# The last two stages of a two-block model kernel on one Trainium2 core: scattered gates, gathered expert rows, and a reordered scan

## The chip, the cores and the metric

The kernel runs on one core of one Trainium2 chip. The metric is the device time of one execution in microseconds (us); 5435.87 us is the median of three runs of the kernel before. All times of instructions are from one profiled execution.

## What is computed

The program is two transformer blocks on 512 tokens of width 1024. The change touches two of its nine stages. The first is the HGRN2 branch of the second block, a gated linear scan in both directions with 8 heads over 512 tokens and 256 context tokens:

```python
bc = jnp.cumsum(logf, axis=3)                       # per chunk of 64 tokens
scores = jnp.einsum('bhnid,bhnjd->bhnij', q * jnp.exp(bc - ref), k * jnp.exp(ref - bc))
o_intra = jnp.einsum('bhnij,bhnjv->bhniv', jnp.where(incl, scores, 0.0), v)
def step(S, xs):                                    # over the chunks
    o_c = einsum(qd_c, S);  S = tot_c[..., :, None] * S + einsum(kd_c, v_c)
o = _rmsnorm(o_f + _flip(o_b), norm_w) * jax.nn.silu(gate)
```

The second is `_peer`, a product-key mixture with 16,384 experts of one row each:

```python
q = (t @ w_query).reshape(n_tok, P_HEADS, 2, P_DQ)           # 8 heads, 2 halves of 128
sc = jnp.einsum('thcd,hckd->thck', q, sub_keys)              # 128 scores per half
# top 16 of each half, top 16 of their 256 sums: 16 experts a head, 128 a token
experts = (e1 * P_NKEYS + e2); gates = jax.nn.softmax(top_s)
act = jax.nn.gelu(einsum('td,tkd->tk', t, expert_u[experts])) * gates
y = einsum('tk,tkd->td', act, expert_v[experts])
```

The output is then a residual sum and an RMS norm. All is float32. Large matrix products are made with three products of float32r parts (high times high, low times high, high times low).

## The kernel before, in words

`program` runs nine phases one after the other; each is a block of five instruction streams (TensorE = PE, VectorE = DVE, ScalarE = ACT, GpSimd = POOL, SyncE = SP) that meet at semaphores. `Marks` and `Steps` are counters of named steps on one semaphore (`mark` raises it, `after` waits for it); `need` is a wait that is left out when its value isn't positive. `split_matmul` (lines 84 to 86) makes the three products.

**scan_phase** (line 2181) goes through periods; in period p it works on head p, prepares head p+1 and finishes earlier heads. On ACT: `decays` and `keys` of head p, `square_out` of head p-1, `sigmoids` of p+1, `gates` of p-1, `values` and `logs` of p+1, `log_out` of p-1, and in the next period the exponential that makes `inv`. On PE: `turn_keys` and `scores` of head p, direction 0; `outputs` of head p-1 (32 small products and 16 wider ones into the bank `out`); `turn_keys` direction 1; `updates` 0, `scores` 1, `updates` 1; `sums` of p-1; `turn_values` of p+1. On DVE: `norm` and `gated` of p-2, `decayed` (kd, ke, qe) of p, `visible` 0 (pt, qd), `states` 0 (eleven dependent steps), `visible` 1, `lengths` of p+1, `states` 1, `sums_of_logs` of p+1 in both directions. `visible` waits until `outputs` of the head before has read pt. POOL only makes constants (the semaphore `made` reaches 12) and is then idle.

**peer_phase** (line 2689) is dense: every token is multiplied with every expert, and a gate matrix of zeros and gates selects. The work is a line of units; a unit is a 128 x 1024 tile against the 1024 x 512 tokens, 8 times `split_matmul`, 24 products of 512 columns. Units 0 to 63 are 8 heads of 2 query tiles and 6 tiles of expert_u; units 64 to 143 are the other 80 tiles of expert_u; units 144 to 271 are the 128 tiles of expert_v. For each unit SP loads 512 KB into `raw` (4 slots), ACT cuts the high part (`cut`, L3112), DVE makes the low part (`low`, L2771), PE multiplies. ACT takes the result of a u unit through Gelu (L3117), and SP stores 256 KB to `hidden` in DRAM.

- Heads (units 0 to 63): after the third unit of a head PE makes the 8 score products (L3051). DVE finds the top 16 with MAX8, FIND_INDEX8 and MATCH_REPLACE8, then key numbers and gates, with eight `low`s between these steps, in an order written out by hand.
- Units 64 to 67, then a transposition of keys and gates, then units 68 to 131 with the gate matrix: for every token DVE makes two one-hot rows (L2860, L2863), PE multiplies them (L3070, 128 columns), ACT copies four tokens' results at a time into `stage` (L3157), SP stores them in 8 pieces of 4 MB to `gate_matrix`.
- Units 132 to 143 without it. SP waits for the last pieces before it loads gates.
- Units 144 to 271: SP loads per unit the v tile (512 KB), `hidden` (256 KB) and, for four units at once, the gates (1 MB). DVE multiplies hidden and gate (L2888), ACT copies the high part (L3178), DVE makes the low part (L2892), PE adds 24 products of 512 columns into eight banks.
- The end: residual (L2916), squares, 8 products with ones (L3105), mean, square root, reciprocal (L2921), output (L2923), stores.

POOL makes constants at the start of the stage and does nothing else in it. Loops run as hardware loops (`rounds`, `Fori`) on all engines.

What orders the u part is one line of the heads' loop in SP and DVE: `need(eng, cut_low, k - 3)` before the load of unit k, `need(products, k - 3)` before its cut, `need(taken, k - 3)` before its products. So a tile is loaded about four units before its use and cut about three.

## Time and profile before

| | us |
|---|---|
| median of 3 runs (5435.79 to 5437.25) | 5435.87 |
| profiled execution, its own time | 5440.96 |
| its span, first to last instruction | 5439.2 |
| PE busy in the span | 4832.4 (89%) |
| DVE busy | 3114.6 (57%) |
| ACT busy | 2083.3 (38%) |
| POOL busy | 65.8 (1%) |
| DRAM traffic, mean | 179 GB/s |

Matmuls are pipelined, so that the busy time of one (0.39 us for 512 columns) is longer than the distance between two; the distance is read from the starts in a timeline. Idle time of an engine is put down to the engine that released it.

### The profile page before, as it was taken

The numbers are of one execution on the slowest core, as the hardware profiler recorded it, in microseconds if no ns is written. First come the engines' busy times: TensorE is split into PE (matmuls) and PEld (weight loads), VectorE is DVE, ScalarE is ACT, GpSimd is POOL, SyncE is SP. The second block draws the span as 40 slices with busy tenths as digits, with TensorE's granted clock in tenths as the row PEclk, the third lists the DMA queues.
The fourth block names the chain that finished last, engine by engine and source line by source line (L and its number), as shares of the span: only waits on it lengthen the run. The fifth ranks groups of instructions, "written<-read, shape, count | busy, mean of one in ns | idle before, by whom it ended". The sixth has DMA issues, their size and how long they took to land. (4 is left out here: it accounts for less than half of the span.)

```text
span 5439.2 us, 67843 instructions
## 1 busy us (share of the span) xinstructions
PE 4832.4 (89%) x24244; PEld 3935.6 (72%) x24244; DVE 3114.6 (57%) x5040; ACT 2083.3 (38%) x2398; POOL 65.8 (1%) x137
## 2 busy tenths in 40 slices
PE   8926799999999569999799975677999999899998
PEld 3923477877877458878699965533888888788887
DVE  0062388888888642233688856512887666344444
ACT  1000267767767301111455545411333444322222
POOL 1000100000000100000000000000000000000000
PEclk9557899999999779999799986688999999999999
DMA  8412599999999623244111011142333454666663
GB/s 345 147 39 91 203 355 367 371 364 367 369 365 368 248 112 109 106 137 141 55 34 36 28 40 47 37 157 102 124 127 127 173 200 170 221 196 191 197 192 120
DMA packets 256059, 976.23 MB, mean 179 GB/s; under 512 B 27060, under 2 KB 63492, under 8 KB 202212
## 3 DMA queue, kind: packets, MB, share of 16 engines
q1 hardware_dynamic: 248516, 923.74, 47.5%
q0 software_dynamic: 7392, 50.50, 2.3%
q8 instruction: 92, 1.51, 0.1%
q14 instruction: 59, 0.48, 0.0%
HBM read 799.87 MB, written 174.28 MB: 179 GB/s over the span
## 5 line engine op out<-in xcount | busy, mean ns | idle before, releaser
L84 PE MATMUL peer_bank<-peer_t_high,peer_high 128*128 128x512 f32 x2176 | 856.4, 394 | 49.4 <-DVE peer_low L2771 35.8
L86 PE MATMUL peer_bank<-peer_t_high,peer_low 128*128 128x512 f32 x2176 | 849.9, 391 | 0.0
L85 PE MATMUL peer_bank<-peer_t_low,peer_high 128*128 128x512 f32 x2176 | 848.2, 390 | 0.0
L2771 DVE TENSOR_TENSOR peer_low<-peer_raw,peer_high 128x1024 fp32r<-128x1024 f32 x272 | 332.6, 1224 | 622.0 <-ACT peer_high L3112 622.0
L1076 DVE TENSOR_TENSOR moe_low<-moe_raw,moe_high 128x2048 fp32r<-128x2048 f32 x256 | 574.6, 2286 | 55.9 <-ACT moe_high L984 53.0
L84 PEld LDWEIGHTS peer_bank<-peer_t_high,peer_high 128*128 128x128 f32 x2176 | 409.9, 188 | 133.1 <-issue 50.6
L984 ACT ACTIVATE moe_high<-moe_raw 128x2048 fp32r<-128x2048 f32 x256 | 478.3, 1906 | 3.7 <-PE moe_up_bank L894 2.0
L3112 ACT ACTIVATE peer_high<-peer_raw 128x1024 fp32r<-128x1024 f32 x272 | 287.0, 1056 | 486.2 <-PE peer_bank L86 481.0
L86 PEld LDWEIGHTS peer_bank<-peer_t_high,peer_low 128*128 128x128 f32 x2176 | 409.5, 188 | 87.0
L85 PEld LDWEIGHTS peer_bank<-peer_t_low,peer_high 128*128 128x128 f32 x2176 | 410.0, 188 | 83.5
L1081 DVE TENSOR_TENSOR moe_low<-moe_raw,moe_high 128x2048 fp32r<-128x2048 f32 x128 | 293.0, 2289 | 66.4 <-ACT moe_high L989 66.4
L3117 ACT ACTIVATE peer_gelu<-peer_bank 128x512 f32<-128x512 f32 x128 | 76.5, 598 | 458.9 <-PE peer_bank L86 458.8
L989 ACT ACTIVATE moe_high<-moe_raw 128x2048 fp32r<-128x2048 f32 x128 | 244.3, 1909 | 0.9 <-DMA moe_raw<-w_down 0.8
L892 PE MATMUL moe_gate_bank<-moe_high,moe_x_high 128*128 128x512 f32 x512 | 210.0, 410 | 11.9 <-DVE moe_low L1076 11.9
L892 PE MATMUL moe_gate_bank<-moe_low,moe_x_high 128*128 128x512 f32 x512 | 201.1, 393 | 0.0
L892 PE MATMUL moe_up_bank<-moe_high,moe_x_high 128*128 128x512 f32 x512 | 201.1, 393 | 0.0
L894 PE MATMUL moe_up_bank<-moe_high,moe_x_low 128*128 128x512 f32 x512 | 200.8, 392 | 0.0
L892 PE MATMUL moe_up_bank<-moe_low,moe_x_high 128*128 128x512 f32 x512 | 200.8, 392 | 0.0
L894 PE MATMUL moe_gate_bank<-moe_high,moe_x_low 128*128 128x512 f32 x512 | 200.1, 391 | 0.0
L170 PE MATMUL mix_bank<-mix_silu_c,mix_ada_w 128*128 128x2 f32 x768 | 164.0, 353 | 5.2 <-ACT mix_silu_c L484 5.2
L170 PEld LDWEIGHTS mix_bank<-mix_silu_c,mix_ada_w 128*128 128x128 f32 x768 | 163.9, 333 | 6.0 <-ACT mix_silu_c L484 6.0
L77 DVE CAST zin_both_w_high<-zin_both_w 128x1024 fp32r<-128x1024 f32 x40 | 27.8, 694 | 242.5 <-DMA zin_both_w<-w_in 242.5
(535 smaller groups left out, 9170.1 us busy)
## 6 DMA issues: line engine op xcount, KB each, us to landing
moe_raw<-w_gate_up SPq DMA_DIRECT2D x256, 1024.0 KB, 6.8
moe_raw<-w_down SPq DMA_DIRECT2D x128, 1024.0 KB
peer_raw<-expert_u SPq DMA_DIRECT2D x128, 512.0 KB, 3.7
peer_raw<-expert_v SPq DMA_DIRECT2D x128, 512.0 KB, 3.5
hidden<-peer_gelu SPq DMA_DIRECT2D x128, 256.0 KB
gate_matrix<-peer_stage SPq DMA_DIRECT2D x8, 4096.0 KB, 12.3
peer_stage<-gate_matrix SPq DMA_DIRECT2D x32, 1024.0 KB, 7.6
peer_stage<-hidden SPq DMA_DIRECT2D x128, 256.0 KB, 3.4
```

The costliest lines, as they stand in the source:

```text
L84: pe.matmul(out, wh, xh, start=start, stop=False)
L85: pe.matmul(out, wh, xl, start=False, stop=False)
L86: return pe.matmul(out, wl, xh, start=False, stop=stop)
L170: last = pe.matmul(out, self.slots[:, n, c], x, **flags)
L892: pe.matmul(out[:], sh[:, c], w[:, part][:, q * 512:(q + 1) * 512], start=False, stop=False, skip_group_check=True)
L894: last = pe.matmul(out[:], sl[:, c], wh[:, part][:, q * 512:(q + 1) * 512], start=False, stop=stop, skip_group_check=True)
L984: act.activation(high[:, gu_slot[j]], raw[:, gu_slot[j]], ACT.Copy).then_inc(gu_high, 1)
L989: act.activation(high[:, dn_slot[j]], raw[:, dn_slot[j]], ACT.Copy).then_inc(dn_high, 1)
L1076: v.tensor_tensor(low[:, slot], raw[:, slot], high[:, slot].bitcast(F32), ALU.subtract).then_inc(gu_low, 1)
L1081: v.tensor_tensor(low[:, slot], raw[:, slot], high[:, slot].bitcast(F32), ALU.subtract).then_inc(dn_low, 1)
L2771: v.tensor_tensor(low_part[:, slot], raw[:, slot], high[:, slot].bitcast(F32), ALU.subtract).then_inc(cut_low, 1)
L3112: act.activation(high[:, slot], raw[:, slot], ACT.Copy).then_inc(cut_high, 1)
```

## The change

It has three parts.

1. **Scan stage.** `outputs` and `sums` of head p now run at the end of period p instead of in the middle of period p+1; `out` is copied to SBUF (`oc`) by a new ACT instruction per head, and `norm` reads that copy. PE makes `updates` 0 before `turn_keys` 1, and `turn_values` before `updates` 1; `updates` leaves out the last chunk. ACT makes `logs` before `values` and `square_out` last. DVE makes `sums_of_logs` 0 before `states` 1. POOL writes zeros to the whole of `gate_matrix`, 32 DMAs of 768 KB.
2. **Peer stage, 384 dense columns.** Expert units (256 of 272) work on the first 384 tokens. Query units keep 512. `hidden` and `gate_matrix` have rows of 384, 192 KB per tile. The one-hot rows, their products, their copies and stores are gone. Instead DVE makes, after each head's keys, the cell number of each (token, expert) pair (three small instructions: pair, cell, expert), and POOL adds each gate to its cell with an indirect DMA of 128 elements of 4 bytes: 16 x 3 per head, 384 in all. Before a head's scatters POOL waits for all scatters of the heads before. SP waits for all scatters before it loads gates.
3. **The last 128 tokens.** POOL gathers, for each of the 128 experts of a token, the row of expert_u and later that of expert_v (128 rows of 4 KB per DMA, 256 DMAs, ring of 6 buffers). DVE makes the dot product with one instruction per gathered u tile and adds a v tile times its gate with another; ACT makes Gelu. Of the 128 dots 112 stand before unit 144, spread over units 69 to 145, the other 16 in the first 16 v units; one v row stands in each v unit. At the end PE transposes the sum into the last 128 columns. The tail makes the root with Ln and Exp on ACT, without reciprocal. All loops of the peer stage are unrolled.

The core of the diff:

```diff
+DENSE = 3 * P
@@ scan_phase
+            pool.memset(zeros[:], 0.0).then_inc(made, 1)
+            for n in range(PEER_KEYS // 4):
+                pool.dma_start(d["gate_matrix"][4 * n:4 * n + 4].rearrange("m e t -> e m t"), zeros[:]).then_inc(gates_cleared, 16)
+            pool.wait_ge(gates_cleared, 16 * PEER_KEYS // 4)
...
                 AO.mark("sq", h, act.activation(sq[:], ob[:], ACT.Square))
+                AO.mark("oc", h, act.activation(oc[h % 2][:], ob[:], ACT.Copy))
...
-                if head(p - 1):
-                    square_out(p - 1)
                 if head(p + 1):
                     sigmoids(p + 1)
                 if head(p - 1):
                     gates(p - 1)
                 if head(p + 1):
-                    values(p + 1)
                     logs(p + 1)
                 if head(p - 1):
                     log_out(p - 1)
+                if head(p + 1):
+                    values(p + 1)
+                if head(p):
+                    square_out(p)
...
                 if head(p):
                     turn_keys(p, 0)
                     scores(p, 0)
-                if head(p - 1):
-                    outputs(p - 1)
-                if head(p):
+                    updates(p, 0)
                     turn_keys(p, 1)
-                    updates(p, 0)
                     scores(p, 1)
-                    updates(p, 1)
-                if head(p - 1):
-                    sums(p - 1)
                 if head(p + 1):
                     turn_values(p + 1)
+                if head(p):
+                    updates(p, 1)
+                    outputs(p)
+                    sums(p)
...
                     lengths(p + 1)
+                    sums_of_logs(p + 1, 0)
                 if head(p):
                     states(p, 1)
                 if head(p + 1):
-                    sums_of_logs(p + 1)
+                    sums_of_logs(p + 1, 1)
@@ peer_phase, DVE
+        place_u = lambda j: j if j < EARLY else EARLY + 2 * (j - EARLY) + 1
+        place_v = lambda j: EARLY + 2 * j if j < TOPK else EARLY + TOPK + j
+        due = lambda k: (k - LATER - 4) * EARLY // (VBASE - LATER - 3)
...
+                V.mark("pair", h, v.scalar_tensor_tensor(pair[:], key2[:], float(PEER_KEYS), key1[:], ALU.mult, ALU.add))
+                V.mark("cell", h, v.scalar_tensor_tensor(cell[:, :, head(h)], pair[:, 0:TD], float(DENSE),
+                                                         token[:, 0:TD].unsqueeze(2).to_broadcast([P, TD, TOPK]), ALU.mult, ALU.add))
+                V.mark("expert", h, v.tensor_copy(expert[:, head(h)], pair[:, TD]))
...
+            def dot(j):
+                n = place_u(j)
+                v.wait_ge(gathered[n % RING], 16 * (n // RING + 1))
+                v.scalar_tensor_tensor(ring[:, n % RING], ring[:, n % RING], 1.0, tok[:], ALU.mult, ALU.mult,
+                                       accum_out=dots[:, j:j + 1]).then_inc(used, 1)
+            for k in range(LATER + 5, VBASE + 2):
+                low(k)
+                for j in range(due(k - 1), due(k)):
+                    dot(j)
...
+            for m in range(PEER_KEYS):
+                if VBASE + 2 + m < LAST:
+                    low(VBASE + 2 + m)
+                if m + 2 < PEER_KEYS:
+                    low_hidden(m + 2)
+                if m + 3 < PEER_KEYS:
+                    gating(m + 3)
+                row(m)
+                if m < TOPK:
+                    dot(EARLY + m)
@@ peer_phase, SP
+                if k == VBASE:
+                    sp.wait_ge(scattered, 16 * HEADS * TOPK * TD)
+                    for m in range(4):
+                        load_gated(m)
@@ peer_phase, POOL
+            def scatter(h, k, t):
+                pool.indirect_dma_start(out=cells, out_offset=at_cell, in_=gate[:, t, h * TOPK + k:h * TOPK + k + 1], in_offset=None,
+                                        compute_op=ALU.add).then_inc(scattered, 16)
+            def gather(rows, j, n):
+                need(pool, used, n - RING + 1)
+                pool.indirect_dma_start(out=ring[:, n % RING], out_offset=None, in_=rows,
+                                        in_offset=bass.IndirectOffsetOnAxis(ap=expert[:, j:j + 1], axis=0)).then_inc(gathered[n % RING], 16)
+            for h in range(HEADS):
+                V.after(pool, "gates", h)
+                need(pool, scattered, 16 * TOPK * TD * h)
+                for k in range(TOPK):
+                    for t in range(TD):
+                        scatter(h, k, t)
+                    if h == 4 and k < RING:
+                        gather(u_rows, k, place_u(k))
+                    if h > 4:
+                        for n in range(2):
+                            j = RING + (h - 5) * 2 * TOPK + 2 * k + n
+                            gather(u_rows, j, place_u(j))
+            for j in range(RING + 6 * TOPK, EARLY):
+                gather(u_rows, j, place_u(j))
```

## Rows read from the trace of the kernel before

**Rows 1.** Windows by stage: scan, heads, rest of u, v, tail; columns in the first line.
```profile
core 0: us, PE busy (x) PEld busy (x) DVE busy (x) ACT busy (x) POOL busy (x), PEclk, DMA share, GB/s
3222.00:3549.00 327.00, 189.01 (x1440) 162.16 (x1440) 190.35 (x342) 161.57 (x240) 2.55 (x13) 0.61 0.15 49
...
3803.00:4166.00 363.00, 363.00 (x1668) 302.95 (x1667) 293.36 (x1032) 129.69 (x208) 0.00 (x0) 1.00 0.39 129
4166.00:4720.00 554.00, 540.34 (x2890) 464.15 (x2889) 331.76 (x1108) 249.52 (x291) 0.00 (x0) 0.99 0.50 178
4720.00:5416.00 696.00, 696.00 (x3068) 576.13 (x3066) 303.28 (x376) 196.61 (x249) 0.00 (x0) 1.00 0.59 188
5416.00:5440.00 24.00, 8.03 (x18) 2.46 (x16) 14.79 (x18) 6.95 (x10) 0.00 (x0) 0.76 0.23 87
```
**Rows 2.** Timeline, PE: products of 512 columns, v stage, two high-by-high ones three apart.
```profile
5000.01 0.39 PE L84 MATMUL peer_bank<-peer_t_high,peer_high 128*128 128x512 f32 x1
...
5000.69 0.39 PE L84 MATMUL peer_bank<-peer_t_high,peer_high 128*128 128x512 f32 x1
```
**Rows 3.** The same view, input stage, products of 256 columns, two apart.
```profile
2200.75 0.28 PE L84 MATMUL zin_context<-zin_hT_high,zin_both_w_high 128*128 128x256 f32 x1
...
2200.98 0.28 PE L86 MATMUL zin_context<-zin_hT_high,zin_both_w_low 128*128 128x256 f32 x1
```
**Rows 4.** DVE's longest wait in the heads' stretch, 3803 to 4166: total, times, longest.
```profile
DVE peer_tick L2790 <- PE peer_bank L3051: 36.8, 8, 4.6
```
**Rows 5.** Timeline, DVE in head 1: its first step and its gates.
```profile
3850.93 0.16 DVE L2790 TENSOR_TENSOR peer_tick<-peer_tick 128x1 f32<-128x1 f32 x1 [4.64 <-PE peer_bank L3051]
...
3887.85 0.22 DVE L2849 TENSOR_TENSOR peer_chosen<-peer_eg,peer_esum 128x64 f32 x1
```
**Rows 6.** POOL's indirect DMAs by source line: the scatters, and the gathers' landing.
```profile
L682 POOL DMA_INDIRECT rows<-route_htok,route_desti x16: 962/962/1071, 556.9 to 576.0; - x16
...
DMA to landing us min/median/max: 11.3/11.4/11.6
```
**Rows 7.** Timeline of the gathers from where DVE is busy beside them.
```profile
1877.32 5.24 DVE L1214 SCALAR_TENSOR_TENSOR combine_acc<-combine_got,combine_gates,combine_acc 128x1024 f32<-128x1024 f32 x4
1878.26 1.15 POOL L1272 DMA_INDIRECT combine_got<-expert_rows,combine_dest  x1 [0.30 <-issue]
1879.71 1.01 POOL L1272 DMA_INDIRECT combine_got<-expert_rows,combine_dest  x1 [0.30 <-issue]
1881.03 1.02 POOL L1272 DMA_INDIRECT combine_got<-expert_rows,combine_dest  x1 [0.30 <-issue]
```
**Rows 8.** A plain small DMA of POOL, by source line.
```profile
L406 POOL DMA_DIRECT2D mix_colsa<-conv_a_b x1: 554/554/554, 2.6 to 2.6; - x1
```
**Rows 9.** Timeline, from the last u unit to the first v unit.
```profile
4715.52 1.35 DVE L2888 TENSOR_TENSOR peer_stage<-peer_stage 128x512 f32<-128x512 f32 x2 [8.56 <-DMA peer_stage<-hidden]
...
4719.19 0.63 PE L84 MATMUL peer_bank<-peer_t_high,peer_high 128*128 128x512 f32 x1
```
**Rows 10.** Groups of the low part and the gating product, 3500 to 5440.
```profile
L2771 DVE TENSOR_TENSOR peer_low<-peer_raw,peer_high 128x1024 fp32r<-128x1024 f32 x272 | 332.6, 1224 | 622.0 <-ACT peer_high L3112 622.0
...
L2888 DVE TENSOR_TENSOR peer_stage<-peer_stage 128x512 f32<-128x512 f32 x128 | 87.5, 684 | 8.7 <-DMA peer_stage<-hidden 8.6
```
**Rows 11.** Windows: first block's expert stage, and beside the gathers; GB/s stands last.
```profile
900.00:1000.00 100.00, 98.28 (x448) 79.32 (x447) 88.54 (x67) 69.86 (x54) 0.00 (x0) 1.00 0.95 367
...
1863.00:1883.00 20.00, 0.00 (x0) 0.00 (x0) 5.88 (x8) 0.00 (x0) 15.19 (x16) 0.50 1.01 383
```
**Rows 12.** Timeline of one period of the scan stage.
```profile
3384.92 0.95 DVE L2507 TENSOR_TENSOR gla_kd<-gla_k,gla_e 128x768 f32<-128x768 f32 x1
...
3388.40 2.08 PE L2438 MATMUL gla_out<-gla_pt,gla_v 128*128 128x128 f32 x8
...
3395.20 0.73 DVE L2519 COPY_PREDICATED gla_pt<-gla_mask,gla_scores 128x512 f32<-128x512 uint32 x1 [5.10 <-PE gla_out L2442]
...
3422.41 0.95 DVE L2507 TENSOR_TENSOR gla_kd<-gla_k,gla_e 128x768 f32<-128x768 f32 x1
```

More of the change, by code:

```diff
@@ new lines, in peer_phase @@
+        expert = s.sb("expert", [P, HEADS * TOPK], U32)
+        tok, y = s.sb("tok", [P, D]), s.sb("y", [P, D])
+        dots, acts = s.sb("dots", [P, HEADS * TOPK]), s.sb("acts", [P, HEADS * TOPK])
+        ring = s.sb("ring", [P, RING, D])
+        tT = early[:, 0:DC * SEQ].rearrange("p (c t) -> p c t", t=SEQ)
+        gated_tiles = early[:, 0:10 * DENSE].rearrange("p (a t) -> p a t", t=DENSE)
+        hid, gates, prod = gated_tiles[:, 0:4], gated_tiles[:, 4:8], gated_tiles[:, 8:10]
+        whole = shared[:].rearrange("p (a t) -> p a t", t=SEQ)
@@ L2909, in _, with gating @@
-            rounds(v, PEER_KEYS // VG - 1, groups)
-            groups(PEER_KEYS // VG - 1, last=True)
+                V.mark("gates", h, v.tensor_tensor(gate[:, :, head(h)], eg[:], esum[:].unsqueeze(2).to_broadcast([P, TT, TOPK]), ALU.mult))
+                low(h * 8 + 12)
+            def gating(m):
+                slot = m % 4
+                v.wait_ge(gates_l[slot], 16 * (m // 4 + 1))
+                v.wait_ge(hid_l[slot], 16 * (m // 4 + 1))
+                need(v, hid_low, m - 1)
+                v.tensor_tensor(prod[:, m % 2], hid[:, slot], gates[:, slot], ALU.mult).then_inc(gated, 1)
@@ new lines, in weigh, with row @@
+            def weigh(h):
+                v.wait_ge(acted, h + 1)
+                v.tensor_tensor(acts[:, head(h)], acts[:, head(h)], gate[:, TD, head(h)], ALU.mult).then_inc(weighed, 1)
+            def row(j):
+                n = place_v(j)
+                v.wait_ge(weighed, j // TOPK + 1)
+                v.wait_ge(gathered[n % RING], 16 * (n // RING + 1))
+                v.wait_ge(used, n)
+                if j:
+                    v.scalar_tensor_tensor(y[:], ring[:, n % RING], acts[:, j:j + 1], y[:], ALU.mult, ALU.add).then_inc(used, 1)
+                else:
+                    v.tensor_scalar(y[:], ring[:, n % RING], acts[:, j:j + 1], None, ALU.mult).then_inc(used, 1)
@@ L2935, in store_u @@
[L2935 removed]
+                sp.dma_start(raw[:, k % 4], source(k)).then_inc(unit_l[k % 4], 16)
+            def store_u(k):
+                m = u_tile(k)
                 sp.wait_ge(taken, k + 1)
[L2937 to L2941 removed]
@@ L3000, in groups @@
[L3000 to L3007 removed]
+                sp.dma_start(d["hidden"][m], gel[:, m % 2]).then_inc(hid_stored[m % 2], 16)
@@ new lines, in load_gated @@
+            def load_gated(m):
+                need(sp, gated, m - 3)
+                sp.dma_start(gates[:, m % 4], d["gate_matrix"][m]).then_inc(gates_l[m % 4], 16)
+                sp.wait_ge(hid_stored[m % 2], 16 * (m // 2 + 1))
+                sp.dma_start(hid[:, m % 4], d["hidden"][m]).then_inc(hid_l[m % 4], 16)
+            sp.dma_start(tT, d["tT"]).then_inc(t_l, 16)
+            for k in range(LAST):
+                if k == VBASE:
+                    sp.wait_ge(scattered, 16 * HEADS * TOPK * TD)
+                    sp.wait_ge(tok_made, 2)
+                    for m in range(4):
+                        load_gated(m)
+                load(k)
+                if k == 1:
+                    sp.dma_start(keys, d["keysT"]).then_inc(k_l, 16)
+                if 4 <= k < VBASE + 4 and not is_query(k - 4):
+                    store_u(k - 4)
+                if k >= VBASE + 4:
+                    load_gated(k - VBASE)
+                if k == VBASE + 8:
+                    V.after(sp, "gates", HEADS - 1)
@@ L3099, in _ @@
-            groups(0, first=True)
-            with pe.Fori(1, PEER_KEYS // VG - 1) as i:
-                groups(i)
-            groups(PEER_KEYS // VG - 1, last_round=True)
+            pe.wait_ge(made, 7)
+            for c in range(DC):
+                last = pe.transpose(bank[6 + c // 4][:, c % 4 * P:(c % 4 + 1) * P], tT[:, c, DENSE:SEQ], ident[:])
+            last.then_inc(turned, 1)
+            for k in range(VBASE):
+                if k < LATER and k % 8 == 3:
+                    h = k // 8
+                    if h == 0:
+                        pe.wait_ge(k_l, 16)
+                    pe.wait_ge(taken, h * 8 + 2)
+                    V.after(pe, f"r{TT - 1}1", h - 1)
+                    for t, c in ((t, c) for c in range(2) for t in range(TT)):
+                        last = pe.matmul(score[c][:, t], qs[:, c, t * P:(t + 1) * P], keys[:, h * 2 + c], start=True, stop=True)
+                    T.mark("scores", h, last)
+                unit(k)
@@ new lines, in _ @@
+            V.after(pe, f"r{TT - 1}1", HEADS - 1)
+            pe.wait_ge(tok_made, 2)
+            for m in range(PEER_KEYS):
+                k = VBASE + m
+                slot = k % 4
+                pe.wait_ge(cut_low, k + 1)
+                pe.wait_ge(hid_low, m + 1)
+                for c in (4, 5, 6, 7, 0, 1, 2, 3):
+                    if m == 0 and c == 0:
+                        pe.wait_ge(taken, VBASE)
+                    part = slice(c * P, (c + 1) * P)
+                    last = split_matmul(pe, bank[c][:, 0:DENSE], (high[:, slot, part], low_part[:, slot, part]), (hh[:, m % 4], hl[:, m % 4]),
+                                        start=m == 0, stop=m == PEER_KEYS - 1)
+                last.then_inc(products, 1)
@@ L3115, in take_u, with take @@
+            def take(k):
                 act.wait_ge(products, k + 1)
-                need(act, hid_stored[half], m)
-                act.activation(gel[:, half], bank[slot][:], ACT.Gelu).then_inc(taken, 1)
+                if is_query(k):
+                    T.after(act, "scores", k // 8 - 1)
+                    act.activation(qs[:, k % 8], bank[k % 4][:], ACT.Copy).then_inc(taken, 1)
+                else:
+                    m = u_tile(k)
+                    need(act, hid_stored[m % 2], 16 * (m // 2))
+                    act.activation(gel[:, m % 2], bank[k % 4][:, 0:DENSE], ACT.Gelu).then_inc(taken, 1)
```

550 lines of the change are left out of this document (203 added, 347 removed).

## The prediction

> **What bounds the kernel now.** I read the windows by stage first. The v stage takes 696 us with PE busy in all of it, the heads 363 us likewise, and the rest of the u part 554 us with 540 busy, at a full granted clock of 1.00; POOL does nothing in any of them and DRAM carries 129 to 188 GB/s [rows 1]. So the peer stage is bound by PE. The scan stage is something else: no engine is busy for 60% of its 327 us, and PE's granted clock is 0.61 on average, that is, mostly its lower level of 1.2 GHz. It is a chain of waits.
>
> The timeline of PE gives the price of a product. Three of 512 columns take 5000.69 - 5000.01 = 0.68 us, 0.227 each [rows 2]; two of 256 columns take 0.23 us, 0.115 each [rows 3]. Halfway is 0.171 for 384 columns. A unit of 24 products is 5.44 us now and would be 4.1 after; I use 4.15. 256 of 272 units are shorter by 1.3 us: 333 us at most from this alone.
>
> Then I looked at what else stands in a head. DVE begins a head at 3850.93 and has its gates at 3887.85 [rows 5], 37 us of a period of 45.3 (363 / 8). Of the other 8 us it waits 4.6 for the scores, 36.8 us in 8 heads [rows 4].
>
> **The change, term by term** (against the profiled execution, span 5439.2 us, time 5440.96).
>
> *Heads.* PE needs 2 x 5.44 + 6 x 4.15 + 1.8 for the scores (45.3 - 8 x 5.44 now) = 37.6 us. DVE needs its 37 us, 0.6 for pair, cell and expert (three instructions near the 0.22 of the gates' product), 1.2 for the last low part [rows 10], and can take back the 1 us it waits for the exponentials: about 38. So PE and DVE are level, and DVE has the last word by little. 8 x 38 = 304 us instead of 363. This alone would be 59 us, if something waited for it.
>
> *POOL.* It is new in this stage, and I think it takes over as the bound. An indirect DMA is 0.96 us with 0.30 us between two; where DVE was busy beside it the starts are 1.45 and 1.32 apart [rows 6, 7]. I take 1.32 for scatters and gathers alike. The kernel before has no adding scatter and none of 4 bytes. The nearest row is the scatter of 128 rows, same number of indices, which I take. Bounds: from below the plain small DMA, 0.55 [rows 8] and no gap; from above 2 x 0.96 + 0.30 = 2.2, if an add has to write its read side twice, for source and destination.
> Up to the first v unit POOL issues 384 scatters and 112 gathers, in one line. It starts at the gates of head 0, 3805 + 38 = 3843 (3805 is where the first scores are done: 3803.4 and 1.8). 496 x 1.32 = 655 us; each head but the first waits until all scatters of the last have landed, 7 x 4 us (the gathers' landing of 11.4 us [rows 6] was behind 512 KB each, a scatter moves 512 bytes; bounds 2 and 11): 28 us. The last gather is issued at 4526. PE alone would be at the 68th unit at 3803 + 304 and at the end of the u units 77 x 4.15 later, at 4427, so POOL is late by 100 us: the gathers of heads 5 to 7 stand between the scatters, the first dot waits until POOL has done head 4 (3843 + 240 x 1.32 + 16 + 6 x 1.32 = 4184, while DVE is there by 4110), and DVE's low parts are queued behind the dots. PE then starves, unit by unit.
>
> *From the last gather to the first v unit.* Landing, the last dots, SP's loads of gates, hidden and tile, gating, high and low part. Before, DVE waits 8.6 us for these loads, and from its first gating (4715.52) to PE's first v product (4719.19) it is 3.7 us more, 12.3 in all [rows 9]. With a landing in front I take 20 (bounds 13 and 35): the v stage begins at 4546, 173 us earlier than now.
>
> *v stage.* Per unit PE 4.15. DVE: low part 1.22, two products of 384 columns at 0.55 (0.68 for 512 less a quarter of the 0.54 that 512 columns more cost) [rows 10], one v row at 1.31 (5.24 / 4 [rows 7]): 3.65. In the first 16 units a dot comes on top, 1.31 and some 0.15 for its sum: 5.1, over PE by 1 us. DRAM: tile 512, gathered rows 512, hidden and gates 192 each, 1408 KB = 1.44 MB, in 4.15 us 347 GB/s. Rates of 367 and 383 are to be had [rows 11], but with nothing left over, and here stands random 4 KB and 1.5 KB traffic. I take 16 x 5.1 + 112 x 4.25 = 558 us (bounds: 4.15 everywhere, 531; 4.8, 614), against 696. POOL issues one gather per unit, 1.3 us, hidden.
>
> *Tail.* Ends 23 us after the last product now. Reciprocal (3.35) and mean (0.7) leave, eight transposes and one more table load come: -2 us.
>
> *Scan.* Before, the outputs of the last head run from 3388.40 to 3395.1 between a head's kd and its pt, and DVE waits 5.1 us for them; a period is 3422.41 - 3384.92 = 37.5 us [rows 12]. After, they run at the end of the period, where half of them (direction 0) lies beside DVE's states; the other half, square and copy (3.2 + 0.6 + 0.6) come before ACT's next exponentials, since ACT is in order, while DVE is at the second sum of logs (3.4 us). The first sum of logs (3.4 us) moves in front of states 1, into time in which DVE waited. Following the chain through gives 32 us per period. 7 x 5.5 = 38, and some 8 at the end, where the head's outputs no longer need a period of their own. Against it stand 25 MB of zeros on POOL's queue: 25.2 MB / 367 GB/s = 69 us of the DMA engines in the first two or three periods, beside loads of 1.5 MB a period that are issued a period ahead. I charge 5. Sum -41 (bounds -15, if the new order only halves the gain; -55).
> The moved instructions leave the queue of SP as it was. POOL waits for the zeros to land, with nothing queued behind; the stage lasts 290 us, so this costs nothing. The unrolled loops cost nothing by themselves: the scan stage is unrolled already.
>
> **Sum.** v stage ends 4546 + 558 = 5104; tail 21; less 41: span 5084. The profiled time is 1.8 above its span and 5.1 above the median of the runs: 5086 - 5 = **5081 us** as a median.
>
> **A rule against it.** Beside a DVE instruction with two SBUF inputs POOL's instruction went from 0.95 to 1.15 and 1.01, never more [rows 7]. The Trainium skill (SBUF — State Buffer, Who interferes with whom) says that such an instruction and a GpSimd instruction that reads SBUF exclude each other for the whole of the instruction, and whoever comes second is blocked. By that rule the trace's 0.2 us would be a mild case; the rival "blocked" below is what it would be at full size.
>
> **Rivals.**
> 1. *The read side of the add costs* (1.5 to 2.2 us per scatter). Every 0.1 us more is 38 us, since POOL is the bound: 5150 at 1.5, 5419 at 2.2. For it: an add has to read its destination, and no row shows one. Against it: the instruction's time may go by indices, 128 in each. 0.17.
> 2. *Blocked.* If each of 496 POOL instructions waited for half of a 1.2 us DVE instruction, 0.6 x 496 = 298 us: 5379. Against it rows 7. 0.05.
> 3. *Cheaper scatters* (0.55 to 1.1). POOL leaves the path at about 1.1 us per instruction (100 us / 496 = 0.2 below 1.32), and PE and DRAM bound the u part: up to 100 us less, 4981. 0.10.
> 4. *DRAM bounds* the v stage at 300 GB/s: 4.8 us per unit, 112 x 0.55 = 62 more: 5143. For it the 347 GB/s needed, against it rows 11. 0.08.
> 5. *Slower: the adds are slow to land.* All scatters of a head have to land before the next head's. If the DMA engines make each 4-byte add by itself, reading, adding and writing before the next, each engine has 8 per scatter; at 0.4 us an add a scatter takes 3.2 us, 384 x 1.9 us over the forecast: 5810. It decides from 2.25 us per scatter. Against it: the chip moves 128-index scatters of 4 KB rows at 1.27 us each. For it: nothing in the trace reads before it writes. 0.09.
> 6. *It does not do what it says:* PE was not the bound of the v stage. Rows 1 and 2 exclude it.
>
> The forecast itself has 0.51.
>
> **Range and chances.** 4960 holds rival 3 and the better end of the scan; 5330 holds rival 4 and two thirds of rival 1. Outside stand rivals 5 and 2 and the rest of 1, about 0.19. A measurement of this kernel can tell about 0.2%, 11 us, from no change. Faster: the forecast, 2, 3, 4 and nearly all of 1: 0.89. Slower: rival 5 and the end of 1: 0.09. Same: 0.02.
>
> **What would show it.** In the changed profile: products of 384 columns 0.17 us apart; POOL with 640 indirect DMAs, without a break from 3843 less the scan's gain to the first v unit; DVE waiting for gathered rows (ring) in the u part, and PE idle behind low parts; a stall of DVE of some 70 us at the first dot; heads of 38 us; v units of 4.2 to 4.3 us after the first 16, at about 340 GB/s; periods of 32 us in the scan. It is wrong if the starts of two scatters are not 1.2 to 1.4 us apart, if DVE's heads stay at 45 us, or if the v units are near 5 us.

## The result and the profile after

The kernel after takes **5359.32 us** (median of 4 runs, 5356.09 to 5364.82), the kernel before 5436.56 in the same runs: ratio 0.9856, 95% interval 0.9841 to 0.987, 1.4% faster. The forecast was 5081 with a range from 4960 to 5330. The sign is right, the size is not: 77 us came of the 355 forecast, and the time lies above the range. The profiled execution took 5357.13 us, span 5355.4, so the sum of the prediction (5084) is short by 271 us.

The windows by stage, as in [rows 1]: heads (first scores to the gates of the last head), rest of u, v stage, tail.

```profile
core 0: us, PE busy (x) PEld busy (x) DVE busy (x) ACT busy (x) POOL busy (x), PEclk, DMA share, GB/s
...
3767.10:4070.80 303.70, 302.26 (x1669) 285.54 (x1668) 294.23 (x1054) 125.26 (x210) 214.83 (x123) 1.00 0.60 144
4070.80:4789.50 718.70, 381.12 (x1848) 364.59 (x1846) 226.93 (x314) 111.96 (x163) 582.66 (x380) 0.78 0.63 165
4789.50:5333.30 543.80, 538.20 (x3071) 537.13 (x3072) 443.25 (x541) 186.63 (x255) 227.51 (x139) 0.99 0.96 349
5333.30:5355.40 22.10, 8.94 (x27) 3.43 (x25) 10.75 (x16) 8.92 (x12) 0.00 (x0) 0.82 0.26 95
```

The heads went from 363 to 304 us and the v stage from 696 to 544, both much as forecast. The second row holds the loss: 719 us, with PE busy in 381 of them, and POOL in 583. A product of 384 columns takes what halfway between [rows 2] and [rows 3] said, 4999.67 to 5001.23 for nine:

```profile
4999.67 0.33 PE L84 MATMUL peer_bank<-peer_hidden_high,peer_high 128*128 128x384 f32 x1
...
5001.23 0.33 PE L84 MATMUL peer_bank<-peer_hidden_high,peer_high 128*128 128x384 f32 x1
```

POOL was 21% of the span busy, for 1%. By line it heads the chain that ended last (by engine PE has 13% of it and POOL 10%):

```profile
POOL gate_matrix L3015 8%; PE peer_bank L84 4%; PE peer_bank L86 4%; PE peer_bank L85 4%; POOL peer_ring L3020 2%; DMA peer_ring<-expert_u_rows,peer_expert 1%; DMA peer_raw<-expert_v 1%; DVE peer_ring L2895 1%; DMA peer_early<-hidden 0%; DVE peer_low L2794 0%; PE peer_bank L3072 0%; DMA gate_matrix<-peer_gate,peer_cell 0%; DMA peer_early<-tT 0%; DVE peer_y L2908 0%; PE peer_bank L3095 0%
```

So the first thing to look at was the price of POOL's instruction. By source line (min/median/max ns), the scatters, and the gathers of u and of v rows:

```profile
L3015 POOL DMA_INDIRECT gate_matrix<-peer_gate,peer_cell x384: 1539/1557/3802, 3805.6 to 4745.3; - x192
...
L3020 POOL DMA_INDIRECT peer_ring<-expert_u_rows,peer_expert x128: 938/997/2041, 4210.7 to 4860.5; - x128
L3020 POOL DMA_INDIRECT peer_ring<-expert_v,peer_expert x128: 938/1677/2640, 4767.0 to 5308.7; - x128
```

No scatter is under 1.54 us, where [rows 6] has 0.96. The group of them on the page of the profile gives their mean:

```profile
L3015 POOL DMA_INDIRECT gate_matrix<-peer_gate,peer_cell x384 | 656.1, 1709 | 205.8 <-issue 125.4
```

At 1.709 on the mean there must be a second effect on top; it shows in the v rows, whose median is 1.68 with a minimum of 0.94. The timeline of a head and of a v unit shows what stands beside the long ones:

```profile
3817.70 1.55 POOL L3015 DMA_INDIRECT gate_matrix<-peer_gate,peer_cell  x1 [0.30 <-issue]
3819.55 3.80 POOL L3015 DMA_INDIRECT gate_matrix<-peer_gate,peer_cell  x1 [0.30 <-issue]
3823.66 1.55 POOL L3015 DMA_INDIRECT gate_matrix<-peer_gate,peer_cell  x1 [0.31 <-issue]
...
3819.38 1.41 DVE L2829 TENSOR_TENSOR peer_shared<-peer_top 128x256 f32<-128x256 f32 x4
3820.71 1.22 DVE L2794 TENSOR_TENSOR peer_low<-peer_raw,peer_high 128x1024 fp32r<-128x1024 f32 x1
...
5000.45 1.22 DVE L2794 TENSOR_TENSOR peer_low<-peer_raw,peer_high 128x1024 fp32r<-128x1024 f32 x1
5000.81 1.68 POOL L3020 DMA_INDIRECT peer_ring<-expert_v,peer_expert  x1 [2.48 <-DVE peer_y L2908]
```

The scatter at 3819.55 is the one that has DVE's sums for the candidates and a low part beside it, with two inputs each; it ends 3.80 us later. The gather at 5000.81 starts inside a low part that hands over at about 5001.6, and ends 0.9 us after that: as if it had stood still until then. In the whole stage the 163 scatters with no DVE instruction beside them take 1.565 on the mean, the 69 such gathers 0.98.

What followed from it, in DVE's and PE's waits from 4070 to 4790 (total, times, longest):

```profile
DVE peer_ring L2895 <- DMA peer_ring<-expert_u_rows,peer_expert: 478.8, 76, 141.9
PE peer_bank L84 <- DVE peer_low L2794: 326.8, 50, 134.7
```

DVE waits for gathered rows, 142 us for the first of them, and PE behind it for low parts: the chain forecast, but twice as long.

### The profile page after: what moved, and what is told of

Its sections match the earlier page's. It is cut to its first block and busy times, and to the rows that moved or that the text cites. A ratio compares the mean times of both kernels' runs of the same rounds, so it can differ in the third digit from the quotient of the medians.

```text
span 5355.4 us, 62778 instructions
## 1 busy us (share of the span) xinstructions
PE 4472.7 (84%) x23192; PEld 3793.6 (71%) x23192; DVE 3146.1 (59%) x4430; ACT 1936.2 (36%) x2287; POOL 1117.1 (21%) x811
## 5 line engine op out<-in xcount | busy, mean ns | idle before, releaser
L3015 POOL DMA_INDIRECT gate_matrix<-peer_gate,peer_cell x384 | 656.1, 1709 | 205.8 <-issue 125.4
L84 PE MATMUL peer_bank<-peer_t_high,peer_high 128*128 128x384 f32 (+1 forms) x1152 | 421.7, 366 | 328.1 <-DVE peer_low L2794 328.0
L85 PE MATMUL peer_bank<-peer_t_low,peer_high 128*128 128x384 f32 (+1 forms) x1152 | 412.1, 358 | 0.0
L86 PE MATMUL peer_bank<-peer_t_high,peer_low 128*128 128x384 f32 (+1 forms) x1152 | 411.5, 357 | 0.0
L84 PE MATMUL peer_bank<-peer_hidden_high,peer_high 128*128 128x384 f32 x1024 | 344.7, 337 | 16.5 <-DVE peer_hidden_low L2889 16.5
L85 PE MATMUL peer_bank<-peer_hidden_low,peer_high 128*128 128x384 f32 x1024 | 344.1, 336 | 0.0
L86 PE MATMUL peer_bank<-peer_hidden_high,peer_low 128*128 128x384 f32 x1024 | 343.9, 336 | 0.0
L3020 POOL DMA_INDIRECT peer_ring<-expert_v,peer_expert x128 | 214.1, 1673 | 290.6 <-DVE peer_y L2908 280.5
L86 PEld LDWEIGHTS peer_bank<-peer_t_high,peer_low 128*128 128x128 f32 x1152 | 231.2, 201 | 5.2
L84 PEld LDWEIGHTS peer_bank<-peer_hidden_high,peer_high 128*128 128x128 f32 x1024 | 193.8, 189 | 17.9 <-issue 17.3
```

Of the source, the lines that this page charges most:

```text
L84: pe.matmul(out, wh, xh, start=start, stop=False)
L85: pe.matmul(out, wh, xl, start=False, stop=False)
L86: return pe.matmul(out, wl, xh, start=False, stop=stop)
L3015: pool.indirect_dma_start(out=cells, out_offset=at_cell, in_=gate[:, t, h * TOPK + k:h * TOPK + k + 1], in_offset=None, compute_op=ALU.add ...
L3020: pool.indirect_dma_start(out=ring[:, n % RING], out_offset=None, in_=rows, in_offset=bass.IndirectOffsetOnAxis(ap=expert[:, j:j + 1], axi ...
```

## Experiments

Each run is compared with the kernel before on the same chip. The times of after and its variants, in us, as they stand to one another:

| kernel | median | ratio to before, 95% interval | v stage starts, first product |
|---|---|---|---|
| after | 5359.3 | 0.9856 (0.9841 to 0.987) | 4789.5 |
| scatters write, not add | 5259.7 | 0.9669 (0.965 to 0.9688) | 4697.3 |
| two of three tiles scattered | 5130.2 | 0.9431 (0.9412 to 0.945) | 4561.3 |
| low part by one-input DVE instruction | 5336.2 | 0.981 (0.979 to 0.9829) | 4770.4 |
| low part by ACT | 5314.2 | 0.9767 (0.9742 to 0.9793) | 4739.1 |
| 32 early dots | 5275.6 | 0.9697 (0.968 to 0.9713) | 4656.3 |
| 64 early dots | 5311.8 | 0.9763 (0.9743 to 0.9782) | 4717.4 |
| first head plain | 5341.3 | 0.9816 (0.9798 to 0.9833) | 4778.3 |
| 32 early dots, first head plain | 5269.3 | 0.9676 (0.9658 to 0.9694) | 4652.7 |
| 24 early dots, first head plain | 5269.9 | 0.9678 (0.966 to 0.9697) | 4644.2 |

**Is it the add?** The kernel after with one argument less:

```diff
-                                        compute_op=ALU.add).then_inc(scattered, 16)
+                                        ).then_inc(scattered, 16)
```

> The 384 scatters write their gate instead of adding it (where a token has the same expert from two heads, only the last head's gate stays in the cell; all else is computed). Theory A, the add makes POOL's instruction long: a scatter falls from 1.55 us alone to about 0.96, like the scatter of the kernel before, its start-to-start time from 1.85 to about 1.3; 384 x 0.55 = 211 us leave POOL, the v stage begins near 4581 instead of 4792, and the time is about 5150. Theory B, the 4-byte row and the index into single cells make it long: 1.55 stays, and the time is 5359 within 10.

By source line:

```profile
L3015 POOL DMA_INDIRECT gate_matrix<-peer_gate,peer_cell x384: 966/972/2021, 3806.4 to 4652.3; - x192
```

Theory A holds for POOL's instruction: 0.97, and 0.979 on the mean for those with no DVE instruction beside them, against 1.565. The 4-byte row and the index into single cells cost nothing. The time fell only half as far as it expected, 5260 and not 5150, for a reason that neither theory had. The longest waits of ACT and of SP from 3806 and 3840 on, PE and ACT in the timeline of the second head, and two windows:

```profile
ACT peer_gelu L3111 <- DMA merge_pb_w<-w_pb: 283.7, 16, 49.7
...
SPq L2968 <- ACT peer_gelu L3111: 286.1, 33, 50.3
```
```profile
3929.61 0.48 PE L84 MATMUL peer_bank<-peer_t_high,peer_high 128*128 128x384 f32 x1 [2.32 <-issue]
3932.41 0.48 PE L85 MATMUL peer_bank<-peer_t_low,peer_high 128*128 128x384 f32 x1 [2.32 <-issue]
...
3945.03 0.49 ACT L3111 ACTIVATE peer_gelu<-peer_bank 128x384 f32<-128x384 f32 x1 [49.67 <-DMA merge_pb_w<-w_pb]
```
```profile
3900.00:3940.00 40.00, 7.17 (x15) 4.60 (x16) 1.35 (x7) 0.00 (x0) 29.13 (x31) 0.50 0.02 0
...
3950.00:3962.00 12.00, 12.00 (x56) 10.09 (x55) 11.79 (x19) 6.40 (x15) 0.00 (x0) 1.00 0.54 187
```

While POOL issues plain scatters in a row, one each 1.27 us, PE makes one product in 1.4 to 2.8 us: 15 of them in 40 us. These gaps lie inside a unit of 24 products, where the code waits for nothing, and the profile names no wait for them ("issue"). ACT's 50 us are the wait for such a unit's last product. The DMA that the profile puts them down to isn't the cause: no transfer is under way (0 GB/s from 3900 to 3940), and SP sends the store of a tile only after ACT's Gelu, for which it waits 286 us in all. The last scatter of the row ends at 3938; by 3945 PE's products follow one another again, and the loads and stores are back. Up to 4420 there are 88 products that start more than 1.2 us after the one before and wait for nothing, 193 us together; in the kernel after there is none. The heads' pitch of 38 us breaks (the gates of the last come at 4289, not 4071), and POOL then waits 68 us for gates and 78 for one dot. Why PE's instructions come so slowly beside plain scatters, and not beside adding ones, is open.

**Is it the add by itself, or the bytes?** The kernel before, with the 16 scatters of [rows 6] adding:

```diff
-                                            in_=htok[:, t, :], in_offset=None).then_inc(scattered, 16)
+                                            in_=htok[:, t, :], in_offset=None, compute_op=ALU.add).then_inc(scattered, 16)
```

> The kernel before, with its 16 scatters of 4 KB rows adding to the cleared rows instead of writing them (every row has one writer, so nothing changes in the result). If the add's 0.59 us is a price per instruction or per index, these go from 0.96 to about 1.55 us each and start 1.85 apart, 9 us in all; if it goes by bytes, 4 KB per index shows as far more than 2 us each. The time is 5437 within 25: beside POOL's 9 us the landing, 11.4 us, can at most double for each of the last ones.

```profile
L682 POOL DMA_INDIRECT rows<-route_htok,route_desti x16: 1557/1562/1702, 555.5 to 583.7; - x16
...
DMA to landing us min/median/max: 6.5/12.6/17.2
```

From 0.962 to 1.562, with rows a thousand times as long: the add costs POOL 0.60 us per instruction of 128 indices, whatever their size. Whether it goes by instruction or by index these runs don't tell, as all have 128. The transfers themselves are another matter. From 565 to 575, before and with the add:

```profile
565.00:575.00 10.00, 10.00 (x25) 4.50 (x24) 1.38 (x2) 0.60 (x1) 7.56 (x9) 1.00 1.00 386
...
565.00:575.00 10.00, 10.00 (x25) 4.50 (x24) 1.38 (x2) 0.60 (x1) 8.44 (x6) 1.00 1.05 207
```

The DMA engines are full in both, and carry 207 instead of 386 GB/s. One run, 5436.5 us.

**Is POOL the bound?** A third of the scatters out (`range(TD)` becomes `range(TD - 1)` in the scatters' loop, and the counts waited for with it).

> Scatters only for two of the three dense tiles of tokens, 256 instead of 384 (tokens 256 to 383 get no gates, so the product of experts for them is left out of the result; all of PE's and DVE's work stays). If POOL is the bound of the u part: 128 x 1.85 = 237 us less, the v stage begins near 4555 and the time is about 5122. Rival, the gathers and dots bound the u part by themselves (landing, ring of 6, DVE's order): under 100 us less, over 5260.

5130, and the v stage starts 228 us sooner: POOL is the bound of the u part, up to the size of this cut. The gathers and dots by themselves allow a start at 4561 or sooner.

**Does DVE hold POOL up?** Two ways to take away the two-input instruction that stands in every unit.

```diff
-                v.tensor_tensor(low_part[:, slot], raw[:, slot], high[:, slot].bitcast(F32), ALU.subtract).then_inc(cut_low, 1)
+                v.tensor_scalar(low_part[:, slot], raw[:, slot], 0.0, None, ALU.mult).then_inc(cut_low, 1)
```

> The low part of a tile is made by a DVE instruction of one SBUF input (times zero) instead of the difference of two, so the third product of each unit multiplies by zero and the result loses the low part; the schedule stays. Contention theory (POOL's indirect DMAs are held up by DVE instructions with two SBUF inputs): the gathers of the v stage, all 1.67 us now, fall to about 1.0 where no other two-input instruction is beside them; the scatters' mean falls from 1.71 towards 1.6 (the sums for the candidates stay two-input), so up to 384 x 0.11 = 42 us and for 112 gathers up to 112 x 0.3 = 34 us leave POOL, and the time is 5270 to 5330. Rival, the stretch is POOL's own or the DMA queue's and only happens to stand beside DVE: gathers stay at 1.6 to 1.7 and the time at 5359 within 10.

The group of the low part, and the v rows:

```profile
L2794 DVE TENSOR_SCALAR peer_low<-peer_raw 128x1024 fp32r<-128x1024 f32 x268 | 185.7, 693 | 23.7 <-ACT peer_high L3102 23.6
```
```profile
L3020 POOL DMA_INDIRECT peer_ring<-expert_v,peer_expert x128: 937/1147/1687, 4749.8 to 5288.4; - x128
```

The time came near to where the theory put it (5336, just above its 5270 to 5330), but not for its reason: scatters that overlap most with this instruction took 1.88 us (53 of them), no less than those beside the two-input one in the kernel after (1.87, 80 of them), and the gathers only fell to 1.15, which fits the shorter instruction. One input is thus no protection, and the run doesn't tell theory from rival. So DVE was taken out of it altogether:

```diff
                 act.activation(high[:, k % 4], raw[:, k % 4], ACT.Copy).then_inc(cut_high, 1)
+                act.activation(low_part[:, k % 4], raw[:, k % 4], ACT.Copy, scale=0.0).then_inc(cut_low, 1)
```

> The kernel after, with the low part of a tile made by ACT (a copy times zero, beside the copy for the high part) and not by DVE, so DVE's 272 two-input instructions of 1.22 us are gone in the peer stage; the third product of each unit multiplies by zero, the low part is left out of the result. The run with a one-input instruction was not clean, since that instruction took 0.69 us and still stood beside stretched gathers. Contention theory: gathers of the v stage fall from 1.64 to about 1.0 to 1.1 (the rows' own instruction and the products remain), the 80 scatters that stood beside the low part lose 26 us, the u part's gathers about 20 to 30, and the v stage begins 40 to 60 us sooner: about 5310. Rival, POOL is stretched by something else that comes at the pitch of the units (a load's DMA, PE): 1.64 stays and the time is 5359 within 10.

```profile
L3018 POOL DMA_INDIRECT peer_ring<-expert_v,peer_expert x128: 935/939/1811, 4728.1 to 5261.2; - x128
```

1.68 became 0.94 with PE and all loads as before and more work on ACT, the scatters' mean went from 1.709 to 1.654, and the time to 5314: the theory's numbers. (Of the 50 us by which the v stage starts sooner, 5 come from the first gates, which a freer DVE has ready at 3800 and not 3805.) What is left of the stretch stands beside the dots (97 scatters, 1.86 on the mean) and the heads' own two-input steps. It matters who is first: in the kernel after 42 of POOL's instructions began with DVE idle and had a two-input instruction begin beside them, and none of them took more than 0.03 us longer than one alone. The Trainium skill (SBUF — State Buffer, Who interferes with whom) names both kinds, the two-input instruction and the one-input copy in its fast mode, and says that the one that comes second is blocked and not slowed; where POOL comes second these traces agree, 1.68 for the gather that starts inside a low part. Where DVE comes second no run shows it: the 133 low parts that start inside one of POOL's instructions take 1.22 us, like the 21 with none beside them. And they differ in one thing: the page takes `tensor_tensor` to spare a GpSimd that makes descriptors, and here it doesn't.

**Fewer gathers in front of the v stage.** `EARLY` says how many of the 128 dots come before it.

```diff
-    RING, EARLY = 6, 7 * TOPK
+    RING, EARLY = 6, 2 * TOPK
+    LATE = HEADS * TOPK - EARLY
...
-    place_v = lambda j: EARLY + 2 * j if j < TOPK else EARLY + TOPK + j
+    place_v = lambda j: EARLY + 2 * j if j < LATE else EARLY + LATE + j
...
-                if m < TOPK:
+                if m < LATE:
                     dot(EARLY + m)
...
-                    if h == 4 and k < RING:
+                    if h == 3 and k < RING:
                         gather(u_rows, k, place_u(k))
-                    if h > 4:
-                        for n in range(2):
-                            j = RING + (h - 5) * 2 * TOPK + 2 * k + n
-                            gather(u_rows, j, place_u(j))
+                    j = RING + ((h - 4) * TOPK + k) // 2
+                    if h > 3 and k % 2 and j < EARLY:
+                        gather(u_rows, j, place_u(j))
```

> Only 32 of the 128 dots (and their gathers) stand before the v stage, the other 96 go one by one into its first 96 units. If POOL is the bound: from its start at 3805 it has 384 x 1.85 = 710 us of scatters, 28 of waits between heads and 32 gathers of about 1.6, 51 us; with 15 us for landing and loads the v stage begins near 4610 (4792 now). The v stage then takes 96 x 4.63 + 32 x 4.17 = 578 us (541 now), and the time is about 5210. Rival, DRAM can't carry 1.97 MB per unit at 4.63 us (425 GB/s): at 400 GB/s a unit is 4.9 us, at 350 5.6 us, and the time 5240 to 5300. Rival, POOL is not the bound: the v stage begins no earlier than 4750, and the time is over 5350.

```profile
4557.00:4656.00 99.00, 0.53 (x4) 0.21 (x2) 6.13 (x9) 3.41 (x6) 70.11 (x48) 0.53 0.38 75
4656.00:5117.00 461.00, 425.48 (x2304) 400.26 (x2304) 421.70 (x575) 142.74 (x199) 277.75 (x188) 0.99 1.03 407
5117.00:5252.00 135.00, 134.21 (x769) 132.78 (x768) 110.07 (x133) 44.86 (x62) 53.60 (x31) 1.00 0.86 324
```
```profile
ACT peer_high L3100 <- DMA peer_raw<-expert_v: 273.2, 84, 11.1
```

84 us better than after, 65 less good than expected. In the first window PE has done all of the u part and stands still while POOL issues its last 48 instructions. I had put a scatter at its median, 1.85 from start to start, where this run's mean is 1.689 + 0.30 = 1.99: 384 x 0.14 = 54 us, and the v stage starts at 4656 and not 4610. In the second, 96 units with a dot take 4.80 us each, at 407 GB/s and a DMA share of 1.03, with ACT waiting for tiles (273 us in it, second fence): here the transfers bound the stage, as the rival said, at a higher rate than its 400. They do so in part of the units only: about half start 4.4 us apart, which is DVE's pitch with a dot, and a third take 4.8 to 6.7 us. The third has no dots: 4.2 us a unit.

> 64 early dots, scatters all adding. Against the run with 32: 32 gathers more on POOL in the u part, 32 x 1.9 = 61 us later to the v stage; 32 units less with a dot, 32 x 0.64 = 20 us less in it: 5275.6 + 41 = about 5316. If the v stage with its dots was limited by DRAM rather than by DVE, the gain in it is the same, so this run only tests the trade.

5311.8, v stage 574 us: the trade is understood from both sides.

**A plain first head.** Its cells hold zeros and a token has no expert twice in one head, so its 48 scatters need no add: `compute_op=ALU.add if h else ALU.bypass`.

> The kernel after, with the 48 scatters of the first head written and not added: its cells are zero and no token has an expert twice in one head, so nothing changes in the result. If the add's 0.59 us is a price on POOL and POOL is the bound: 48 x 0.59 = 28 us less than the kernel after, about 5331, with the first head's scatters over in 70 us instead of 98. Rival, plain scatters hold up the other DMA queue as in the run where all were plain: SP's stores of hidden land up to 50 us late during the first head, the heads' pitch of 38 us breaks, but as POOL is the bound later, less than half of the 28 us is lost.

POOL's waits from 3800 to 3900:

```profile
POOL gate_matrix L3015 <- DVE peer_gate L2877: 88.1, 2, 68.2
ACT peer_gelu L3112 <- PE peer_bank L86: 51.6, 6, 37.2
```

The time fell by 18 us at the median, of the 28 expected. The profiled execution is one of the two longer ones (5346): its v stage starts only 11 us sooner, 4 of them because its first scatter does. The head was over after 48 x (1.015 + 0.30) = 63 us, and then POOL waited 88.1 - 68.2 = 20 us for the next gates, which had been held up as in the first experiment. So the rival is right in its effect and wrong in its cause: SP's stores don't land late, ACT waits up to 37 us for PE, whose products come up to 2.8 us apart here too, 17 of them, until 5 us after the last plain scatter. The rival's "less than half" of the gain is lost at the median, more than half in the profiled execution.

> Both edits: 32 early dots and the first head's scatters plain. 5275.6 less 28: about 5248, if the two gains add.

5269.3 (5254.6 to 5271.9): 6 us below the version with the adds (5272.4 to 5276.4). All four runs lie below those, but on another chip, and the intervals of the ratios overlap. It is 21 us short of the 5248 of two gains that add; PE's slow products are there again.

> As the last with 24 early dots instead of 32. 8 gathers less on POOL in the u part, 8 x 1.9 = 15 us sooner; 8 units more with a dot at 4.80 instead of 4.16 us, 5 us later: 10 us less, about 5238. Rival, rows wait for the second head's dots: no gain.

5269.9: the v stage starts 8.5 us sooner and is 8.4 us longer. The best whole version is thus the one with 32 early dots, 1.6% below the kernel after; what the plain first head adds is at most some 6 us.

**The scan alone.** The kernel before with the new scan stage, without and with the zeros.

```diff
                 if head(p):
                     turn_keys(p, 0)
                     scores(p, 0)
-                if head(p - 1):
-                    outputs(p - 1)
...
+                if head(p):
+                    updates(p, 1)
+                    outputs(p)
+                    sums(p)
```

> The kernel before with nothing but the scan stage's new order, without the zeros. The traces before and after have the first scores of the peer stage 36 us apart. If that is the order's own gain and the zeros cost nothing: 36 us less than before, ratio 0.9934. If the zeros took 5 us as I charged: 41 us less. Rival, part of the 36 comes from elsewhere (the peer stage's own start): under 30 us.

5406.9, ratio 0.9936 (0.9917 to 0.9955): 31 us.

> The same with the 25 MB of zeros written from POOL's queue in the scan stage too (into the gate matrix of this kernel, in pieces of 1.5 KB as in the kernel after; they are overwritten later). 36 us less than before if the trace of after is read rightly; against the run without zeros 0 to 5 us more. Rival, zeros crowd out the loads of z in the first periods: 10 us and more over the run without them.

5404.2, ratio 0.9932 (0.9913 to 0.9952): 34 us. So the order brings 31 to 36 us, and the zeros cost nothing that shows.

## Why the prediction was right in its sign and wrong in its size

**The step that failed is "I take 1.32 for scatters and gathers alike".** It took the nearest row, 128 indices without an add, and made the add itself rival 1 with a chance of 0.17. The starts of two scatters came 1.85 us apart at the median and 2.01 on the mean, outside the 1.2 to 1.4 that the prediction set as its own condition. The account of POOL from its first scatter to its last early gather, from the trace of after: 961 us, of which 384 x 1.709 = 656 are scatters, 112 x 1.195 = 134 gathers, 495 x 0.30 = 149 the gaps, and 23 waits. The prediction had 655 + 28 = 683. The 278 us between them cover the 271 by which the span was missed:

- the add: 384 x 0.60 = 230 us of POOL's time, shown by two runs, one in each kernel. The run without the add gave back only 100 us, since PE's slow products took its place;
- DVE beside POOL: scatters at 1.709 instead of 1.565, 55 us, and gathers at 1.195 instead of 0.98, 24 us. The forecast's 1.32 held 0.06 us of this for each instruction, 30 us; 49 are left. The run with the low part on ACT shows the low part's share of it; that of the dots and of the heads' steps is argued from what stands beside the long ones.

I read [rows 7] as a bound ("never more") where they were only the mild cases: 0.2 us there, up to 2.2 here. The same trace shows why they were mild, in the second of the four DVE instructions that [rows 7] print as one:

```profile
1878.63 1.28 DVE L1214 SCALAR_TENSOR_TENSOR combine_acc<-combine_got,combine_gates,combine_acc 128x1024 f32<-128x1024 f32 x1
```

It ends at 1879.91, and the gather beside it starts at 1879.71. The three gathers of [rows 7] start with 0.34, 0.21 and 0.21 us of a DVE instruction left, and lose 0.21, 0.07 and 0.08; the gather of the v stage at 5000.81 starts with 0.86 left and loses 0.74. It is one rule, a wait for what is left less some 0.13, at a late and at an early start.

POOL's waits came out at 23 us, about half of them between heads, for the 28 forecast there.

**Heads: right.** 37.95 us from head to head for 38.

**The stall at the first dot: right in kind.** 142 us for 70; DVE was there at 4073, and POOL came to the first gather, behind four heads of 92 to 104 us, only at 4211.

**From the last gather to the v stage:** issue at 4764.7, first product at 4789.5, 25 us for 20.

**V stage: right**, 544 us for 558. DVE's instructions are 1.28, 1.22, 0.56 and 0.55, 3.6 for 3.65; units without a dot take 4.16 for 4.25, and the first 16, with one, 4.77 for 5.1. The 4.77 are no sign that the dots cost what I said: thirteen of these sixteen units take 4.16, since DVE's pitch with a dot is 4.41 and it has a lead, and three take 6.6 to 9.0; two of those, from 4821 on, come behind SP's load of 2 MB (`x3`), issued at 4803.7 and landed 18.9 us later, which the sum did not have. 349 GB/s were carried without other loss, so rival 4 is out for this kernel, though it is what limits the version with 96 dots in the v stage.

**Tail: right**, 22.1 us.

**Scan: right in kind.** The first scores come 36 us sooner, for 41 (46 for the order, less 5 for the zeros, which cost nothing): a period is 33.9 us from kd to kd, for 32. In the kernel after:

```profile
3371.18 0.96 DVE L2519 TENSOR_TENSOR gla_kd<-gla_k,gla_e 128x768 f32<-128x768 f32 x1
...
3405.11 0.96 DVE L2519 TENSOR_TENSOR gla_kd<-gla_k,gla_e 128x768 f32<-128x768 f32 x1
```

**The rivals.** Rival 1 is what happened, at 1.85 us from start to start of its 1.5 to 2.2. By its own price that is 384 x 0.53 = 204 us, about 5285; the 5359 need rival 2 as well. That I set the two apart and never together is the second fault: the range ended at two thirds of rival 1, and the sum of both lay outside it. Rival 2 was seen as a tax of 0.6 us on each of 496 instructions, and is one of some 0.16 on the mean, since only those that start within a two-input instruction pay. Rival 3 fell with the price, and rival 6 is out, as the v stage's units fell to PE's 4.16. Rival 5 is excluded: between the last scatter of a head and the first of the next POOL is idle for 2 to 3 us, or not at all, so the adds have landed by then. Its 0.4 us an add was an assumption that no run shows.

## What to carry to other kernels

When one engine issues hundreds of like instructions and is to become the bound, its price per instruction is the forecast: an unmeasured option on that instruction (here the add) deserves the middle of its bounds and not the lower end, and what DVE does beside it belongs in the price. Take an issue rate from the mean start-to-start time of a stretch, not from the median duration. And where an early stage is bound by an issuing engine and a later one is not, move its work there until the later one's limit, here the transfers at 407 GB/s, comes up.

## What the runs showed of the hardware that I had not expected

- `compute_op=add` lengthens POOL's indirect DMA by 0.60 us per instruction of 128 indices, with 4-byte rows (0.979 to 1.565) and with 4 KB rows (0.962 to 1.562) alike.
- The same add on 4 KB rows halves what the full DMA engines carry, 207 for 386 GB/s.
- POOL's indirect DMA stands still when it starts within a two-input DVE instruction, up to 3.80 us for 1.55, and within the 0.69 us `tensor_scalar` on 1024 floats too; if it was there first, it isn't held up. Beside MAX8 and FIND_INDEX8 it takes 1.55 to 1.61, and ACT's copies of the same size do not touch it.
- While plain scatters of single cells are issued every 1.27 us, PE's products come 1.4 to 2.8 us apart instead of 0.17, with the DMA engines 2% busy; beside adding ones, every 1.85 us, they don't. Whether rate or kind decides was not tried.
- After a stall PE starts anew at its lower level: the granted clock is 0.50 to 0.53 (1.2 GHz) in the two windows above in which it starves, and the first products after a gap of 135 us are 0.32 us apart, against 0.17:

```profile
4217.70 0.69 PE L84 MATMUL peer_bank<-peer_t_high,peer_high 128*128 128x384 f32 x1 [134.67 <-DVE peer_low L2794]
...
4219.14 0.52 PE L85 MATMUL peer_bank<-peer_t_low,peer_high 128*128 128x384 f32 x1
4219.46 0.52 PE L86 MATMUL peer_bank<-peer_t_high,peer_low 128*128 128x384 f32 x1
```

As POOL bounds the u part, I take it that this costs nothing there.
